# The last multiplications of the hybrid layer's mixer, from GpSimd to VectorE

## The chip, the cores and the metric

The kernel runs on one core of a Trainium2 chip. A core has TensorE (matrix products into PSUM), VectorE, ScalarE and GpSimd (elementwise work), and SyncE, which here issues most transfers. Each engine takes its own instructions in order, and the engines wait for each other through semaphores. The metric is the device time of one execution in microseconds; lower is better. Where several runs are shown, the median counts.

## The reference, cut to what matters

A network of two transformer layers and one hybrid layer is computed for 512 tokens of width 1024. The hybrid layer projects its input to p, gives slices of p to three mixers, and joins what they return:

```python
y_rwkv = rwkv7_time_mix(p_rwkv, ...)
y_mla = mla_attention(p_mla, ...)
y_gdn = gated_deltanet(p_gdn, ...)
y = jnp.concatenate([y_rwkv, y_mla, y_gdn], axis=-1)
h = h + y @ w_out[l]
```

Two of the mixers are recurrences. Each ends with a normalization of every head of 64 values and a multiplication by a gate:

```python
# rwkv7_time_mix
mean = jnp.mean(y, axis=-1, keepdims=True)
var = jnp.mean(jnp.square(y - mean), axis=-1, keepdims=True)
y = ((y - mean) * lax.rsqrt(var + RWKV_GN_EPS)).reshape(B, S, RWKV_WIDTH)
y = y * gn_g.astype(f32) + gn_b.astype(f32)
y = y + bonus.reshape(B, S, RWKV_WIDTH)
return (y * g.astype(f32)).astype(p.dtype)

# gated_deltanet
o = _rms(o, o_norm_g) * jax.nn.silu(hd(gate).astype(f32))
```

The change concerns the last multiplication of each, by `g` and by `silu(gate)`.

## The kernel before

Activations lie in SBUF transposed: a tile is 128 channels (partitions) by 512 tokens, in float32. The program is a row of stages. A stage allocates its tiles and semaphores, gives each engine a block of instructions, and ends with a barrier of all engines; in the trace, an engine's wait at such a barrier is put down to its sequencer and line 207. The order within a stage is written out by hand: each engine's instructions stand in program order, with a wait on a semaphore ahead of whatever depends on another instruction. The hybrid layer (`hybrid`) runs the stages that prepare both recurrences, then `recurrence` ("rec"), `mixer_ends` ("fin"), `latent` ("mla", the third mixer) and the output projection ("out"), then the feed-forward part.

`mixer_ends` treats six tiles in the order 3, 4, 5, 0, 1, 2. Tiles 0 to 2 are the first recurrence's, 3 to 5 are the gated delta net's. TensorE sums over heads by a product with a constant matrix (into `m_ps` for means, `v_ps` for squares). ScalarE makes the squares, the three gates `sgate` by Silu (semaphore `silued`), and then for each tile a logarithm and an exponential, which give the reciprocal root in `sq` (semaphore `rs_done`). VectorE computes the differences `d`, and then for each tile, as soon as its exponential is there:

- tiles 3 to 5: one instruction, line 2819, `o = y * o_norm * sq`;
- tiles 0 to 2: two instructions, line 2814, `o = d * gn_g * sq`, and, after a wait for it, line 2816, `o = (o + gn_b) + bonus`.

Each tile's last one counts up `o_done`. GpSimd waits for that and multiplies by the gate into `k.H`: line 2833 for tiles 3 to 5, with `sgate`, and line 2831 for tiles 0 and 1, with the gate that lies in `pi`. The sixth tile's multiplication, tile 2's, is VectorE's (line 2823). All operands of lines 2814 to 2833 lie in SBUF. `k.H` is read after the next barrier.

In `latent`, lines 3028 to 3041 are VectorE's first steps, 3047 takes TensorE's projections out of PSUM, 3062 and 3065 are the rotation of positions (3065 also waits for a product that GpSimd makes), and 3085 normalizes a block of attention weights, 4 blocks in each of 4 heads.

Of the kernel before, what the change touches and what calls it, by code (L numbers as in the profile page):

```python
# [19 lines left out]
ALU = mybir.AluOpType  # L20
# [27 lines left out]
MIX_T = 3  # L48
# [219 lines left out]
def linker(eng, sem):  # L268


    count = [0]

    def link(ins):
        ins.then_inc(sem, 1)
        count[0] += 1
        eng.wait_ge(sem, count[0])

    return link
# [1466 lines left out]
R_R, R_K, R_V, R_WA, R_G = 0, 3, 6, 9, 10  # L1745
# [1014 lines left out]
def mixer_ends(k, pi, y):  # L2760

    with Stage(k, "fin") as st:
        NP = 2 * MIX_T
        d = st.sb("d", [P, MIX_T, S])
        sq, o = (st.sb(n, [P, NP, S]) for n in ("sq", "o"))
        sgate = st.sb("sgate", [P, MIX_T, S])
        m_ps, v_ps = st.ps("m_ps", [P, MIX_T, S]), st.ps("v_ps", [P, 5, S])
        mean_done, d_done, squared, var_done, ln_done, rs_done, chain, o_done, out_done, silued = (st.sem(n) for n in (
            "mean_done", "d_done", "squared", "var_done", "ln_done", "rs_done", "chain", "o_done", "out_done", "silued"))

        order = [3, 4, 5, 0, 1, 2]
        with k.nc.Block() as block:
            @block.tensor
            def _(pe):
                for n in range(MIX_T):
                    pe.matmul(m_ps[:, n, :], k.c("heads"), y[n], start=True, stop=True).then_inc(mean_done, 1)
                for q, n in enumerate(order):
                    pe.wait_ge(squared, q + 1)
                    if q == 5:
                        pe.wait_ge(ln_done, 1)  # L2780
                    pe.matmul(v_ps[:, q % 5, :], k.c("heads"), sq[:, n, :], start=True, stop=True).then_inc(var_done, 1)

            @block.scalar
            def _(act):
                for n in order[:MIX_T]:
                    act.activation(sq[:, n, :], y[n], ACT.Square).then_inc(squared, 1)
                for j in range(MIX_T):
                    act.activation(sgate[:, j, :], pi[:, G_GATE + j, :], ACT.Silu).then_inc(silued, 1)
                for n in order[MIX_T:]:
                    act.wait_ge(d_done, n + 1)  # L2790
                    act.activation(sq[:, n, :], d[:, n, :], ACT.Square).then_inc(squared, 1)
                act.preload_act_table_set(LN_EXP)
                for q in range(NP + 1):
                    if q < NP:
                        n = order[q]
                        eps = 1 if n < MIX_T else 0
                        act.wait_ge(var_done, q + 1)
                        act.activation(sq[:, n, :], v_ps[:, q % 5, :], ACT.Ln, scale=1.0 / 64, bias=k.eps[:, eps:eps + 1]).then_inc(ln_done, 1)
                    if q:
                        n = order[q - 1]  # L2800
                        act.wait_ge(ln_done, q)
                        act.activation(sq[:, n, :], sq[:, n, :], ACT.Exp, scale=-0.5).then_inc(rs_done, 1)

            @block.vector
            def _(dve):
                link = linker(dve, chain)
                for n in range(MIX_T):
                    dve.wait_ge(mean_done, n + 1)
                    dve.scalar_tensor_tensor(out=d[:, n, :], in0=m_ps[:, n, :], scalar=-1.0 / 64, in1=y[n],
                                             op0=ALU.mult, op1=ALU.add).then_inc(d_done, 1)  # L2810
                for q, n in enumerate(order):
                    dve.wait_ge(rs_done, q + 1)
                    if n < MIX_T:
                        link(dve.scalar_tensor_tensor(out=o[:, n, :], in0=d[:, n, :], scalar=k.p("gn_g", n), in1=sq[:, n, :],
                                                      op0=ALU.mult, op1=ALU.mult))
                        dve.scalar_tensor_tensor(out=o[:, n, :], in0=o[:, n, :], scalar=k.p("gn_b", n), in1=pi[:, R_K + n, :],
                                                 op0=ALU.add, op1=ALU.add).then_inc(o_done, 1)
                    else:
                        dve.scalar_tensor_tensor(out=o[:, n, :], in0=y[n], scalar=k.p("o_norm"), in1=sq[:, n, :],
                                                 op0=ALU.mult, op1=ALU.mult).then_inc(o_done, 1)  # L2820

                dve.wait_ge(o_done, NP)
                dve.tensor_tensor(k.H[:, order[-1], :], o[:, order[-1], :], pi[:, R_R + order[-1], :], ALU.mult).then_inc(out_done, 1)

            @block.gpsimd
            def _(pool):
                pool.wait_ge(silued, MIX_T)
                for q, n in enumerate(order[:-1]):
                    pool.wait_ge(o_done, q + 1)
                    if n < MIX_T:  # L2830
                        pool.tensor_tensor(k.H[:, n, :], o[:, n, :], pi[:, R_R + n, :], ALU.mult).then_inc(out_done, 1)
                    else:
                        pool.tensor_tensor(k.H[:, 2 + n, :], o[:, n, :], sgate[:, n - MIX_T, :], ALU.mult).then_inc(out_done, 1)


TWO_PI = 2 * math.pi
# [277 lines left out]
def hybrid(k):  # L3114

    with ExitStack() as ctx:
        def sb(name, shape):
            return ctx.enter_context(k.nc.sbuf_tensor(name, shape, F32))

        pi = sb("pi", [P, IN_T, S])  # L3120
        with ExitStack() as ctx2:
            def sb2(name, shape):
                return ctx2.enter_context(k.nc.sbuf_tensor(name, shape, F32))

            bi = sb2("bi", [P, MIX_T, S])
            kr = sb2("kr", [P, MIX_T, TT, 2, P])
            ki = sb2("ki", [P, MIX_T, S])
            pc, el = sb2("pc", [P, MIX_T, NCH]), sb2("el", [P, MIX_T, NCH])
            rows2 = sb2("rows2", [P, S])
            cols = sb2("cols", [P, 120])  # L3130
            mixer_inputs(k, pi, kr, bi, ki, pc, rows2, cols)
            mt, n0 = sb2("mt", [P, 2 * MIX_T, NCH, CHUNK]), sb2("n0", [P, 2 * MIX_T, NCH, CHUNK])
            a, b = slice(0, MIX_T), slice(MIX_T, 2 * MIX_T)
            v, gk, gv = pi[:, R_V:R_V + MIX_T, :], pi[:, G_K:G_K + MIX_T, :], pi[:, G_V:G_V + MIX_T, :]
            rows = [pi[:, R_WA, :], pi[:, R_G, :], rows2]
            chunk_operators(k, "rwc", bi, kr, ki, v, kr, k.H, mt[:, a], n0[:, a], bi, v, pc)
            delta_rows(k, pi, kr, ki, rows, el)
            chunk_operators(k, "gdc", gk, kr, None, gv, ki, k.H, mt[:, b], n0[:, b], gk, gv, el, (rows, cols))
            y = [v[:, i, :] for i in range(MIX_T)] + [gv[:, i, :] for i in range(MIX_T)]
            recurrence(k, mt, n0, [bi[:, i, :] for i in range(MIX_T)] + [gk[:, i, :] for i in range(MIX_T)], (v, gv))  # L3140
        mixer_ends(k, pi, y)
        latent(k, pi)
# [125 lines left out]
```

## Time and profile before

| | |
|---|---|
| median of 3 runs | 2374.66 us |
| the three runs | 2374.49, 2374.66, 2376.17 us |
| the profiled execution | 2374.99 us |
| its span, first to last instruction | 2373.2 us |
| TensorE's mean granted clock | 0.972 |
| TensorE, VectorE, ScalarE busy | 2212.7, 1301.8, 913.2 us |
| GpSimd busy | 142.2 us, 113 instructions |
| stage "fin", from its first matmul to the first work behind its barrier | 1855.4 to 1877.6 us |

Durations and starts come from one profiled execution, whose time is 1.79 us longer than its span. A timeline lists instructions by their start in us from the start of the span; successive ones of one kind are merged, with their number behind x and their common duration. What an engine's idle time waited for stands in square brackets. The granted clock is a share of TensorE's full speed: 1.00 is 2.4 GHz, 0.50 is 1.2 GHz.

### The profile page before, as it was taken

What the parts mean: (1) busy time and instruction counts of PE and PEld (TensorE: products, weight loads), DVE (VectorE), ACT (ScalarE), POOL (GpSimd) and SP (SyncE); (2) the same over time, 40 slices, a digit from 0 to 9 for tenths busy, and PEclk for the clock granted to TensorE, in tenths of its full rate; (3) what the DMA queues carried; (4) which work ended last, traced back from release to release, by engine and by line L of the source; (5) the groups of instructions that cost most, each with busy time, mean ns of one, the idle gap of its engine ahead of it and who ended that gap; (6) DMA issues with size and microseconds to landing.
All of it is one profiled execution on the core that took longest, in us unless ns stands there. A gap on an engine that the chain in (4) does not pass through costs nothing. (4 is left out here: it accounts for less than half of the span.)

```text
span 2373.2 us, 35779 instructions
## 1 busy us (share of the span) xinstructions
PE 2212.7 (93%) x13998; PEld 1749.6 (74%) x13998; DVE 1301.8 (55%) x1703; ACT 913.2 (38%) x1428; POOL 142.2 (6%) x113
## 2 busy tenths in 40 slices
PE   7998999999989998999999999998777689999999
PEld 5786788888866776678888876777756337788887
DVE  5554476663476776386664376874343673533333
ACT  4444432222445565442222355552211452423222
POOL 0000011110000000011110000002222110000000
PEclk9998999999999999999999999999979889999999
DMA  6330333333223220323332323220000002333332
GB/s 229 99 125 18 107 96 99 90 101 96 94 61 107 69 70 26 101 86 97 94 101 98 95 67 94 80 89 2 3 2 3 13 1 72 111 96 96 98 96 71
DMA packets 52583, 186.96 MB, mean 79 GB/s; under 512 B 5712, under 2 KB 5968, under 8 KB 52336
## 3 DMA queue, kind: packets, MB, share of 16 engines
q1 hardware_dynamic: 52176, 184.69, 25.0%
q8 instruction: 87, 1.43, 0.2%
q10 hardware_dynamic: 288, 0.58, 0.1%
q14 instruction: 32, 0.26, 0.0%
HBM read 183.15 MB, written 2.10 MB: 78 GB/s over the span
## 5 line engine op out<-in xcount | busy, mean ns | idle before, releaser
L263 PE MATMUL tail_banks<-tail_r_hi,tail_w_hi 128*128 128x512 f32 x1344 | 529.8, 394 | 7.7 <-DVE tail_r_lo L1648 7.4
L265 PE MATMUL tail_banks<-tail_r_hi,tail_w_lo 128*128 128x512 f32 x1344 | 523.1, 389 | 0.0
L264 PE MATMUL tail_banks<-tail_r_lo,tail_w_hi 128*128 128x512 f32 x1344 | 523.1, 389 | 0.0
L263 PEld LDWEIGHTS tail_banks<-tail_r_hi,tail_w_hi 128*128 128x128 f32 x1344 | 252.2, 188 | 67.8 <-DVE tail_r_lo L1648 7.5
L264 PEld LDWEIGHTS tail_banks<-tail_r_lo,tail_w_hi 128*128 128x128 f32 x1344 | 252.3, 188 | 54.7 <-issue 3.4
L248 DVE TENSOR_TENSOR tail_w_lo<-ring,tail_w_hi 128x1024 fp32r<-128x1024 f32 x168 | 241.5, 1440 | 92.3 <-ACT tail_w_hi L242 89.1
L265 PEld LDWEIGHTS tail_banks<-tail_r_hi,tail_w_lo 128*128 128x128 f32 x1344 | 252.3, 188 | 53.0
L242 ACT ACTIVATE tail_w_hi<-ring 128x1024 fp32r<-128x1024 f32 x168 | 176.7, 1056 | 229.1 <-PE tail_banks L265 226.6
L263 PE MATMUL ff_banks<-ff_r_hi,ff_w_hi 128*128 128x512 f32 x512 | 200.0, 391 | 0.0
L265 PE MATMUL ff_banks<-ff_r_hi,ff_w_lo 128*128 128x512 f32 x512 | 199.2, 389 | 0.0
L264 PE MATMUL ff_banks<-ff_r_lo,ff_w_hi 128*128 128x512 f32 x512 | 199.2, 389 | 0.0
L705 POOL TENSOR_TENSOR tail_mid<-H 128x512 f32 x44 | 60.2, 1368 | 1202.6 <-ACT H L698 828.6
L248 DVE TENSOR_TENSOR ff_w_lo<-ring,ff_w_hi 128x1024 fp32r<-128x1024 f32 x64 | 78.4, 1226 | 61.3 <-ACT ff_w_hi L242 57.9
L263 PEld LDWEIGHTS ff_banks<-ff_r_hi,ff_w_hi 128*128 128x128 f32 x512 | 96.1, 188 | 20.6 <-issue 0.5
L264 PEld LDWEIGHTS ff_banks<-ff_r_lo,ff_w_hi 128*128 128x128 f32 x512 | 96.1, 188 | 20.2 <-issue 0.5
L265 PEld LDWEIGHTS ff_banks<-ff_r_hi,ff_w_lo 128*128 128x128 f32 x512 | 96.1, 188 | 20.0
L256 DVE TENSOR_TENSOR tail_r_lo<-tail_mid,tail_r_hi 128x512 fp32r<-128x512 f32 x44 | 30.4, 692 | 130.3 <-ACT tail_r_hi L252 130.3
L263 PE MATMUL na_acc<-na_r_hi,na_w_hi 128*128 128x512 f32 x192 | 78.1, 407 | 15.5 <-DVE na_r_lo L929 15.5
L263 PE MATMUL in_acc<-in_r_hi,in_w_hi 128*128 128x512 f32 x216 | 91.1, 422 | 0.0
L263 PE MATMUL da_acc<-da_r_hi,da_w_hi 128*128 128x512 f32 x192 | 80.8, 421 | 7.4 <-DVE da_r_lo L1250 7.4
L252 ACT ACTIVATE tail_r_hi<-tail_mid 128x512 fp32r (+1 forms) x44 | 27.7, 630 | 153.1 <-PE tail_banks L265 153.1
L265 PE MATMUL in_acc<-in_r_hi,in_w_lo 128*128 128x512 f32 x216 | 84.9, 393 | 0.0
(476 smaller groups left out, 3578.9 us busy)
## 6 DMA issues: line engine op xcount, KB each, us to landing
ring<-weights SPq DMA_DIRECT2D x315, 512.0 KB, 3.6
na_bias<-window_bias SPq DMA_DIRECT2D x16, 512.0 KB, 5.5
da_rel<-t_rel SPq DMA_DIRECT2D x8, 448.0 KB, 4.0
X<-xT SPq DMA_DIRECT2D x1, 2048.0 KB, 9.0
outT<-X SPq DMA_DIRECT2D x8, 256.0 KB, 2.1
const<-consts SPq DMA_DIRECT2D x1, 1328.5 KB, 14.4
tail_pt<-pT SPq DMA_DIRECT2D x2, 512.0 KB, 3.5
H<-lora ACTq DMA_DIRECT2D x1, 384.0 KB, 2.8
```

Of the source, the lines that this page charges most:

```text
L242: act.activation(self.w_hi[:, c % self.slots, :], k.ring[:, g % RING, :], ACT.Copy).then_inc(self.w_rounded, 1)
L248: dve.tensor_tensor(self.w_lo[:, c % self.slots, :], k.ring[:, g % RING, :], self.w_hi[:, c % self.slots, :].bitcast(F32), ALU.subtract).t ...
L252: act.activation(self.r_hi[:, slot, :], src, ACT.Copy).then_inc(self.rhs_rounded, 1)
L256: dve.tensor_tensor(self.r_lo[:, slot, :], src, self.r_hi[:, slot, :].bitcast(F32), ALU.subtract).then_inc(self.rhs_split, 1)
L263: pe.matmul(psum, hi, self.r_hi[:, rhs_slot, :], start=start, stop=False)
L264: pe.matmul(psum, hi, self.r_lo[:, rhs_slot, :], start=False, stop=False)
L265: return pe.matmul(psum, lo, self.r_hi[:, rhs_slot, :], start=False, stop=stop)
L705: pool.tensor_tensor(mid[:, f + j, :], gelu[:, j, :], value[:, j, :], ALU.mult).then_inc(mid_done, 1)
```

## The change

VectorE now does the multiplication by the gate for all six tiles, each right behind the instruction that makes its `o`. GpSimd's block in this stage is gone. The wait for the Silu gates is now on VectorE, one gate at a time. Nothing else differs.

```diff
--- before.py
+++ after.py
@@ -2818,19 +2818,12 @@
                     else:
                         dve.scalar_tensor_tensor(out=o[:, n, :], in0=y[n], scalar=k.p("o_norm"), in1=sq[:, n, :],
                                                  op0=ALU.mult, op1=ALU.mult).then_inc(o_done, 1)
-
-                dve.wait_ge(o_done, NP)
-                dve.tensor_tensor(k.H[:, order[-1], :], o[:, order[-1], :], pi[:, R_R + order[-1], :], ALU.mult).then_inc(out_done, 1)
-
-            @block.gpsimd
-            def _(pool):
-                pool.wait_ge(silued, MIX_T)
-                for q, n in enumerate(order[:-1]):
-                    pool.wait_ge(o_done, q + 1)
+                    dve.wait_ge(o_done, q + 1)
                     if n < MIX_T:
-                        pool.tensor_tensor(k.H[:, n, :], o[:, n, :], pi[:, R_R + n, :], ALU.mult).then_inc(out_done, 1)
+                        dve.tensor_tensor(k.H[:, n, :], o[:, n, :], pi[:, R_R + n, :], ALU.mult).then_inc(out_done, 1)
                     else:
-                        pool.tensor_tensor(k.H[:, 2 + n, :], o[:, n, :], sgate[:, n - MIX_T, :], ALU.mult).then_inc(out_done, 1)
+                        dve.wait_ge(silued, n - MIX_T + 1)
+                        dve.tensor_tensor(k.H[:, 2 + n, :], o[:, n, :], sgate[:, n - MIX_T, :], ALU.mult).then_inc(out_done, 1)
```

VectorE's rows at the end of the stage "fin", with the lines of each kernel's own file; `fin_` marks the stage's tiles:

```order
 L2809 SCALAR_TENSOR_TENSOR fin_d<-fin_m_ps,pi 128x512 x3
-L2819 SCALAR_TENSOR_TENSOR fin_o<-pi,par,fin_sq 128x512 x3
+L2819 SCALAR_TENSOR_TENSOR fin_o<-pi,par,fin_sq 128x512
+L2826 TENSOR_TENSOR H<-fin_o,fin_sgate 128x512
+L2819 SCALAR_TENSOR_TENSOR fin_o<-pi,par,fin_sq 128x512
+L2826 TENSOR_TENSOR H<-fin_o,fin_sgate 128x512
+L2819 SCALAR_TENSOR_TENSOR fin_o<-pi,par,fin_sq 128x512
+L2826 TENSOR_TENSOR H<-fin_o,fin_sgate 128x512
 L2814 SCALAR_TENSOR_TENSOR fin_o<-fin_d,par,fin_sq 128x512
 L2816 SCALAR_TENSOR_TENSOR fin_o<-fin_o,par,pi 128x512
+L2823 TENSOR_TENSOR H<-fin_o,pi 128x512
```

A multiplication stands between any two tiles now, where VectorE went on to the next tile at once; tiles 0 and 1 have theirs as tile 2 had it.

GpSimd's rows from the end of the stage before "fin" to the stage "mla" (ISA rows belong to the clearing of semaphores between stages):

```order
-L206 ISA x2
-L2825 UNCONDITIONAL_BRANCH
-L2833 TENSOR_TENSOR H<-fin_o,fin_sgate 128x512 x3
-L2831 TENSOR_TENSOR H<-fin_o,pi 128x512 x2
-L2772 UNCONDITIONAL_BRANCH
-L206 ISA
-L3014 UNCONDITIONAL_BRANCH
-L3018 COPY mla_qk<-pi 32x512 x4
-L3022 TENSOR_TENSOR mla_qk<-mla_qk,mla_cs 32x512 x8
-L2873 UNCONDITIONAL_BRANCH
 L206 ISA x3
```

The five multiplications and their block are gone; the rows of "mla" below stand in the changed kernel too, seven line numbers lower.

## Rows read from the trace of the kernel before

**Rows 1.** Page, busy us of two engines, share of the span, instructions.

```profile
PE 2212.7 (93%) x13998; PEld 1749.6 (74%) x13998; DVE 1301.8 (55%) x1703; ACT 913.2 (38%) x1428; POOL 142.2 (6%) x113
```

**Rows 2.** Timeline of TensorE: start us, duration us, engine, instruction [idle before].

```profile
1863.78 1.10 PE L2781 MATMUL fin_v_ps<-fin_sq,const 128*128 128x512 f32 x2 [1.15 <-ACT fin_sq L2798]
1880.11 2.08 PE L2884 MATMUL mla_a_ps<-mla_sq,const 128*128 128x512 f32 x2 [15.24 <-ACT mla_sq L2960]
```

**Rows 3.** Timeline of VectorE, from the first exponential to the barrier.

```profile
1864.76 0.75 DVE L2819 SCALAR_TENSOR_TENSOR fin_o<-pi,par,fin_sq 128x512 f32<-128x512 f32 x1 [5.77 <-ACT fin_sq L2802]
1865.86 2.28 DVE L2819 SCALAR_TENSOR_TENSOR fin_o<-pi,par,fin_sq 128x512 f32<-128x512 f32 x2 [0.34 <-ACT fin_sq L2802]
1868.06 1.75 DVE L2814 SCALAR_TENSOR_TENSOR fin_o<-fin_d,par,fin_sq 128x512 f32<-128x512 f32 x1
1869.85 1.63 DVE L2816 SCALAR_TENSOR_TENSOR fin_o<-fin_o,par,pi 128x512 f32<-128x512 f32 x1
1871.40 0.74 DVE L2814 SCALAR_TENSOR_TENSOR fin_o<-fin_d,par,fin_sq 128x512 f32<-128x512 f32 x1
1872.18 1.63 DVE L2816 SCALAR_TENSOR_TENSOR fin_o<-fin_o,par,pi 128x512 f32<-128x512 f32 x1
1873.74 0.74 DVE L2814 SCALAR_TENSOR_TENSOR fin_o<-fin_d,par,fin_sq 128x512 f32<-128x512 f32 x1
1874.51 1.63 DVE L2816 SCALAR_TENSOR_TENSOR fin_o<-fin_o,par,pi 128x512 f32<-128x512 f32 x1
1876.18 0.69 DVE L2823 TENSOR_TENSOR H<-fin_o,pi 128x512 f32<-128x512 f32 x1
```

**Rows 4.** Instructions of tile fin_o, line 2819: ns min/median/max, first and last start.

```profile
L2819 DVE SCALAR_TENSOR_TENSOR fin_o<-pi,par,fin_sq x3: 737/751/1620, 1864.8 to 1867.4; 128x512 f32<-128x512 f32 x3
```

**Rows 5.** Timeline of GpSimd in the stage "fin".

```profile
1865.66 1.27 POOL L2833 TENSOR_TENSOR H<-fin_o,fin_sgate 128x512 f32<-128x512 f32 x1 [39.75 <-DVE fin_o L2819]
1867.56 3.38 POOL L2833 TENSOR_TENSOR H<-fin_o,fin_sgate 128x512 f32<-128x512 f32 x2 [0.63 <-DVE fin_o L2819]
1871.56 1.70 POOL L2831 TENSOR_TENSOR H<-fin_o,pi 128x512 f32<-128x512 f32 x1 [0.63 <-DVE fin_o L2816]
1873.89 1.70 POOL L2831 TENSOR_TENSOR H<-fin_o,pi 128x512 f32<-128x512 f32 x1 [0.63 <-DVE fin_o L2816]
```

**Rows 6.** Timeline of ScalarE: the second, fifth and sixth of the six exponentials.

```profile
1865.19 0.64 ACT L2802 ACTIVATE fin_sq<-fin_sq 128x512 f32<-128x512 f32 x1
...
1868.45 1.18 ACT L2802 ACTIVATE fin_sq<-fin_sq 128x512 f32<-128x512 f32 x2
```

**Rows 7.** Timeline of VectorE: the first instruction behind the barrier, three merged.

```profile
1877.66 2.37 DVE L3028 TENSOR_SCALAR mla_cg<-pi,par 128x512 f32<-128x512 f32 x3 [0.79 <-PEq L207]
```

**Rows 8.** Windows: us, length, TensorE busy (instructions), granted clock, DMA share, GB/s.

```profile
1880.00:1886.00 6.00, 5.49 (x6) 0.53 0.15 58
...
1916.00:1937.00 21.00, 16.02 (x35) 0.51 0.00 1
...
1960.00:1964.00 4.00, 3.91 (x20) 0.59 0.00 0
...
1970.00:2373.00 403.00, 396.86 (x1738) 1.00 0.31 94
```

**Rows 9.** Timeline of VectorE: the rotation, no pause between.

```profile
1922.18 0.68 DVE L3062 TENSOR_TENSOR mla_t<-mla_a_ps,mla_sn 32x512 f32<-32x512 f32 x1
1922.89 0.68 DVE L3065 TENSOR_TENSOR mla_qk<-mla_qk,mla_t 32x512 f32<-32x512 f32 x1
```

**Rows 10.** Timeline of VectorE: first projection taken out of PSUM.

```profile
1888.51 0.69 DVE L3047 TENSOR_TENSOR mla_qk<-mla_a_ps,mla_rs 96x512 f32<-96x512 f32 x1 [1.74 <-PE mla_a_ps L2898]
```

**Rows 11.** Timeline of VectorE: first normalized block of heads 0, 1 and 3.

```profile
1928.41 0.29 DVE L3085 TENSOR_SCALAR mla_e<-mla_e,mla_inv 128x128 f32<-128x128 f32 x1
...
1937.35 0.29 DVE L3085 TENSOR_SCALAR mla_e<-mla_e,mla_inv 128x128 f32<-128x128 f32 x1
...
1954.09 0.29 DVE L3085 TENSOR_SCALAR mla_e<-mla_e,mla_inv 128x128 f32<-128x128 f32 x1
```

## Prediction, made before the changed kernel had run

> **What bounds the kernel now.** I read four views in this order. The page's busy times show TensorE at 93% of the span and GpSimd at 6% [rows 1]: the kernel is TensorE's, except where TensorE has nothing to do. The timeline of the end of the mixer shows such a place. TensorE's last matmul of the stage "fin" ends at 1863.78 + 1.10 = 1864.88 us, and its next one, in the stage "mla", starts at 1880.11, after 15.24 us of idle time [rows 2]. So in this stretch the time is set by the chain on VectorE, not by TensorE. The third view is VectorE's own timeline: it works from 1864.76 to 1876.18 + 0.69 = 1876.87 with one pause, of 0.34 us [rows 3]. GpSimd is done at 1873.89 + 1.70 = 1875.59 [rows 5], that is 1.28 us before VectorE; ScalarE at 1868.45 + 1.18 = 1869.63 [rows 6]. VectorE is therefore the last to reach the barrier between the stages, and its first instruction behind it starts at 1877.66, 0.79 us later [rows 7]. What moves VectorE's end moves the start of "mla" by as much. The fourth view, the windows, shows whether something behind swallows it: from 1970 us to the end TensorE is busy 396.86 of 403 us [rows 8], so nothing there waits for another clock than TensorE's, and a stage that starts earlier ends the kernel earlier.
>
> **What VectorE and GpSimd do to each other now.** The same instruction has two durations here. The three of line 2819 take 737, 751 and 1620 ns [rows 4]; line 2814 takes 1.75 us once and 0.74 us twice; line 2816 takes 1.63 us three times [rows 3]. The long durations are five, and each of them ends shortly after a GpSimd instruction ends. GpSimd's five end at 1866.93, 1869.27, 1870.94, 1873.26 and 1875.59 (start plus duration; the two merged ones are 3.38 us together) [rows 5]. The long VectorE instructions end at 1867.48, 1869.81, 1871.48, 1873.81 and 1876.14 [rows 3, 4]. The distance is 0.54 or 0.55 us in all five. I read this as follows: a VectorE instruction that takes two operands from SBUF and begins while GpSimd works there waits until GpSimd is done, and only then streams. The short ones of line 2814 began at 1871.40 and 1873.74, 0.16 and 0.15 us ahead of a GpSimd instruction. So the multiplications given to GpSimd are not done beside VectorE's work; VectorE stands still for most of each of them.
>
> **The change, step by step.** (a) Five long instructions become short. At 0.74 us for a free one [rows 3] the excess is 1.62 - 0.74 = 0.88, 1.75 - 0.74 = 1.01 and 3 x (1.63 - 0.74) = 2.67, together 4.56 us less. (b) Five multiplications come to VectorE. The one that it does already, from SBUF to SBUF with GpSimd idle, takes 0.69 us, and starts 0.04 us behind the end of the instruction on which it waits (1876.14 to 1876.18) [rows 3]. So 5 x 0.73 = 3.65 us more. (c) Before an independent instruction VectorE starts 0.08 us before the last has ended (1871.40 against 1871.48) [rows 3]; there is one more such place now, 0.08 us less. (d) The pause before 1865.86, from 1865.51, in which VectorE waited for ScalarE's second exponential [rows 3, 6], is filled by the first multiplication: 0.35 us less. The sum is -4.56 + 3.65 - 0.08 - 0.35 = **-1.34 us**.
>
> Walked forward instead, it is the same: 1864.76 + 0.75 + 0.04 + 0.69 = 1866.24 for the first tile, twice 1.39 for the next two (-0.08 + 0.74 + 0.04 + 0.69), and three times 2.17 for those with two steps ahead of the multiplication (-0.08 + 0.74 + 0.04 + 0.74 + 0.04 + 0.69): 1875.53 instead of 1876.87. ScalarE does not become the bound: its second exponential is ready at 1865.83 and the last at 1869.63 [rows 6], and VectorE wants them at 1866.16 and 1873.28.
>
> (e) Added waits. Behind each wait for o_done stands only VectorE's own next work, and the producer is the instruction just ahead, which the 0.04 us covers. The second wait, for silued, stands before three of the multiplications. ScalarE's gates are computed before its first exponential, so it is satisfied. Two waits in a row, one of them long satisfied, cost nothing visible where the trace has them: line 3065 waits for VectorE's line 3062 and for GpSimd, and starts at 1922.89 behind 1922.18 + 0.68 [rows 9]. I take 0; the upper bound is another 0.04 for each, 0.12 us. (f) GpSimd loses its block and comes to the barrier early; nobody waits for it. Its next work starts with everyone else's. (g) No DMA moves past another: the loads of "mla" are issued by SP behind the same barrier, so they start 1.34 us earlier too.
>
> **A rule weighed.** In the stretch from 1864.76 to 1876.87 VectorE is busy nearly all the time, and the row says that moving work away from it brought it 4.56 us of standing still for 3.65 us of work saved. The Trainium skill, Perfetto Trace Analysis, section Optimizing Scalar/DVE Operations, says that with VectorE saturated it may make sense to offload some work to ScalarE or even GpSimd, and warns that between VectorE and GpSimd it might not help. By its first half this change would lose; by its warning and by the rows it gains. The first half is rival 1 below.
>
> **Rivals.** 1, *the long durations are VectorE's own* (slower than before). If the five long durations stay when GpSimd is idle, only (b), (c) and (d) are left: 3.65 - 0.08 - 0.35 = +3.22 us, 2377.9. It decides where less than 3.22 of the 4.56 us goes away. Against it stands that lines 2819 and 2814 show both durations with one shape. The partial form is stronger: line 2816 is never seen free, 1.63 us three times [rows 3], and could be so by itself. Then 2.67 us of (a) stays, and the sum is +1.33 us, 2376.0. Against it: all three end 0.54 or 0.55 us behind GpSimd, as the other two long ones do. The Trainium skill, SBUF — State Buffer, section SBUF: two separate sides, calls the pair of ports an exclusive lock, held for a whole instruction, on which the loser blocks fully. By that rule line 2816 is a blocked one, and the distances in the trace agree.
>
> 2, *TensorE's clock* (either sign). TensorE's granted clock is 0.53 in 1880 to 1886, at the lower of its two levels (1.2 GHz), 0.51 in 1916 to 1937, and 0.59 in 1960 to 1964 [rows 8]; before each of these it had been idle or partly idle. The whole of "mla" moves by 1.34 us, and where the clock falls and rises may move otherwise. Bounds from the rows. At the start the matmuls run at the lower level; with the full clock the next step of VectorE, which waited 1.74 us for TensorE [rows 10], gains at most that. In 1960 to 1964 TensorE is the bound, and about 3.4 us at the lower level are at most 1.7 us lost. In the heads between, the first one takes 1937.35 - 1928.41 = 8.94 us mostly at the lower level, the next two (1954.09 - 1937.35) / 2 = 8.37 at the full one [rows 11]: 0.57 us a head. So the clock can give at most 1.74 + 1.7 + 0.57 = 4.0 us (2369.3, all three falls gone) and take some 3 x 0.57 = 1.7 us (2375.0).
>
> 3, *the gain does not arrive*: another engine holds the barrier. Nothing speaks for it; the next to arrive is GpSimd at 1875.59, and its work is what the change takes away. It gives 2374.7.
>
> **How the numbers follow.** The profiled execution took 2374.99 us, 1.79 more than its span; with the sum it is 2373.65. The median of the three runs is 0.33 lower, and the forecast is 2374.66 - 1.34 = 2373.3 us. A measurement of this kernel tells about 0.2%, 4.7 us, from no change. Chances: the forecast with clock effects under 2 us 0.78; a clock that moves in its favour by more 0.08, 2370; one against it 0.05, 2375.5; rival 1 in its partial form 0.03, in full 0.02; rival 3 0.04. The range runs from 2370.4 (the forecast, the first clock gain and most of one of the others) to 2375.8 (the forecast, 1.7 us of lost clock and the 0.8 us by which the three runs stand apart from their middle). Faster by over 0.2% needs more than the clock's full gain or something not seen here, 0.06; slower by over 0.2%, 0.05; within, 0.89.
>
> **What would show it.** In the profile after: lines 2819, 2814 and 2816 all at 0.74 to 0.75 us, six multiplications at 0.69 us, VectorE without a pause from 1864.76, its last end near 1875.5, and the first work of "mla" near 1876.3. A line 2816 at 1.63 us with GpSimd idle would prove rival 1. A start of "mla" 1.3 us earlier with an end of the kernel that differs by another amount would be rival 2, and the granted clock would show where. The prediction is wrong if work ahead of 1864 us moves, since nothing there is changed.

## The result, and the profile after

The changed kernel takes 2377.97 us (median of 20 runs, 2375.02 to 2385.74) against 2374.89 us for the kernel before (median of 20 runs, 2370.47 to 2379.10). The ratio is 1.0016, with an interval of 1.0010 to 1.0023: it is slower by 3.1 us by the medians (3.8 by the ratio), where 1.3 us of gain was forecast, and it lies outside the range. Its profiled execution took 2378.00 us with a span of 2376.2.

The stage that was changed does what the prediction said, to a hundredth. VectorE's timeline of the changed kernel: the first of the three tiles with one step ahead of the multiplication, the first and the end of the last of the three with two, and the first work behind the barrier (start us, duration us, line; [idle before]), answering [rows 3]:

```profile
1864.42 0.75 DVE L2819 SCALAR_TENSOR_TENSOR fin_o<-pi,par,fin_sq 128x512 f32<-128x512 f32 x1 [5.77 <-ACT fin_sq L2802]
1865.20 0.69 DVE L2826 TENSOR_TENSOR H<-fin_o,fin_sgate 128x512 f32<-128x512 f32 x1
...
1868.59 0.75 DVE L2814 SCALAR_TENSOR_TENSOR fin_o<-fin_d,par,fin_sq 128x512 f32<-128x512 f32 x1
1869.37 0.75 DVE L2816 SCALAR_TENSOR_TENSOR fin_o<-fin_o,par,pi 128x512 f32<-128x512 f32 x1
1870.16 0.69 DVE L2823 TENSOR_TENSOR H<-fin_o,pi 128x512 f32<-128x512 f32 x1
...
1873.72 0.75 DVE L2816 SCALAR_TENSOR_TENSOR fin_o<-fin_o,par,pi 128x512 f32<-128x512 f32 x1
1874.51 0.69 DVE L2823 TENSOR_TENSOR H<-fin_o,pi 128x512 f32<-128x512 f32 x1
1876.31 2.37 DVE L3021 TENSOR_SCALAR mla_cg<-pi,par 128x512 f32<-128x512 f32 x3 [1.11 <-PEq L207]
```

Line 2816, never seen free before, takes 0.75 us where it took 1.63. From the first exponential to VectorE's last end there are 1875.20 - 1864.42 = 10.78 us, before 12.11: 1.33 us less, forecast 1.34. The barrier behind it takes 0.32 us of that away again: 1.11 us of idle time where [rows 7] has 0.79.

The loss lies behind. The first instruction of "fin" lies 0.34 us earlier in this trace, though nothing ahead of it was changed, so I count from VectorE's first instruction in "fin" (line 2809, at 1856.58 before and 1856.24 after). The table gives the start of VectorE's first instruction of each part, from the timelines, in us from there:

| part | before | after | difference |
|---|---|---|---|
| "mla" begins | 21.08 | 20.07 | -1.01 |
| first projection taken out of PSUM | 31.93 | 29.77 | -2.16 |
| first normalization | 44.87 | 42.71 | -2.16 |
| last step of the rotation | 68.23 | 71.58 | +3.35 |
| head 0, first block | 71.83 | 75.18 | +3.35 |
| head 3, first block | 97.51 | 100.86 | +3.35 |
| output projection | 111.84 | 115.19 | +3.35 |

The rotation of positions takes 5.51 us more, and nothing else takes more: 3.35 us behind the mark less 0.34 ahead of it are the 3.01 us by which the two profiled executions differ. TensorE's windows of both kernels say why (us, length, TensorE busy (instructions), granted clock, DMA share, GB/s). Before:

```profile
1886.00:1902.00 16.00, 14.96 (x36) 1.00 0.00 0
1902.00:1916.00 14.00, 12.08 (x29) 1.00 0.00 1
1916.00:1936.00 20.00, 15.02 (x31) 0.51 0.00 1
```

After:

```profile
1880.00:1886.00 6.00, 5.13 (x10) 0.85 0.00 0
1886.00:1902.00 16.00, 14.91 (x37) 1.00 0.00 0
1902.00:1916.00 14.00, 14.00 (x18) 0.51 0.00 1
1916.00:1936.00 20.00, 16.71 (x26) 0.50 0.01 1
1936.00:1940.00 4.00, 3.89 (x14) 0.52 0.00 0
```

The clock falls to its lower level (1.2 GHz) at 1902.2 instead of 1916.3, 14 us earlier, and rises at 1939.8 instead of 1936.8. (In return it had risen 3.0 us after TensorE's restart in "mla" instead of 5.5, which is the second microsecond gained in the table, and the clock gain that rival 2 named.) At the lower level the matmuls of a rotation step take nearly twice as long (1.91 and 2.02 us for 1.04 and 1.10), and TensorE becomes the bound. TensorE's timeline before, at 1.00:

```profile
1906.40 1.04 PE L2909 MATMUL mla_a_ps<-mla_qk,const 32*32 32x512 f32 x2
1907.38 1.10 PE L2915 MATMUL mla_s_ps<-mla_sq,const 96*96 96x512 f32 x2
1908.40 1.04 PE L2909 MATMUL mla_a_ps<-mla_qk,const 32*32 32x512 f32 x2
1909.38 1.10 PE L2915 MATMUL mla_s_ps<-mla_sq,const 96*96 96x512 f32 x2
1911.06 1.01 PE L2909 MATMUL mla_a_ps<-mla_qk,const 32*32 32x512 f32 x2 [0.58 <-DVE mla_t L3062]
```

After, at 0.50, without a pause:

```profile
1905.36 1.91 PE L2902 MATMUL mla_a_ps<-mla_qk,const 32*32 32x512 f32 x2
1907.20 2.02 PE L2908 MATMUL mla_s_ps<-mla_sq,const 96*96 96x512 f32 x2
1909.15 1.91 PE L2902 MATMUL mla_a_ps<-mla_qk,const 32*32 32x512 f32 x2
```

From one rotation matmul to the next there are 1909.15 - 1905.36 = 3.79 us, where before they were 2.45 us apart once VectorE set the pace (1911.06 to 1913.51). VectorE, which had no idle time in these steps before, now waits in each step for GpSimd's product, and GpSimd for TensorE:

```profile
1904.97 0.68 DVE L3058 TENSOR_TENSOR mla_qk<-mla_qk,mla_t 32x512 f32<-32x512 f32 x1 [0.51 <-POOL mla_qk L3015]
1908.78 0.68 DVE L3058 TENSOR_TENSOR mla_qk<-mla_qk,mla_t 32x512 f32<-32x512 f32 x1 [0.79 <-POOL mla_qk L3015]
```

### The profile page after: what moved, and what is told of

It is laid out like the page before. It is cut to its first block and busy times, and to the rows that moved or that the text cites. A ratio compares the mean times of both kernels' runs of the same rounds, so it can differ in the third digit from the quotient of the medians.

```text
span 2376.2 us, 35781 instructions
## 1 busy us (share of the span) xinstructions
PE 2219.7 (93%) x13998; PEld 1750.1 (74%) x13998; DVE 1297.2 (55%) x1708; ACT 913.2 (38%) x1428; POOL 133.9 (6%) x108
```

## The experiments

Two theories. **C, the clock**: the change gains in its own stage and loses because TensorE's clock falls at another point of the rotation, since "mla" starts at another moment. **G, the change itself**: something that it does (GpSimd idle for 50 us, instructions at other addresses) makes "mla" slower, whenever it starts.

### The start of "mla" put back: e1, e2

Behind the last multiplication of "fin", VectorE does two more, whose results are not used:

```diff
+dve.tensor_tensor(sq[:, 3, :], o[:, 3, :], o[:, 3, :], ALU.mult).then_inc(extra, 1)
+dve.tensor_tensor(sq[:, 4, :], o[:, 4, :], o[:, 4, :], ALU.mult).then_inc(extra, 1)
```

In the changed kernel:

> The changed kernel with two further VectorE multiplications of 128x512 behind the last one of the stage fin (their results are not used). They take 2 x 0.61 us, so the stage mla starts about where it starts in the kernel before. Theory C (clock): the loss of 3 us is not made by the change in its own stage, which gains its 1.3 us, but by TensorE's clock, which falls at 1902 instead of 1916 us because mla starts at another moment. Then this kernel is near the kernel before, 2374 to 2376 us, and the clock falls in the second half of the rotation. Theory G (the change itself, such as GpSimd being idle longer or the instructions lying elsewhere): the loss stays and the delay is added to it, 2379.2 us.

Measured: 2375.49 us median of 12 runs; ratio to the kernel before, beside it, 1.0003 (0.9994 to 1.0012). More work made the changed kernel faster by 2.5 us. Its trace repeats the kernel before within 0.13 us at every mark: "mla" at 20.96, first projection 31.81, last rotation step 68.10, head 0 71.70, output projection 111.77 us after the first instruction of "fin" (before: 21.08, 31.93, 68.23, 71.83, 111.84). The clock falls at 1917.8, 59.7 us behind that mark as before. Its windows:

```profile
1886.00:1902.00 16.00, 15.13 (x35) 0.96 0.00 0
1902.00:1916.00 14.00, 11.93 (x29) 1.00 0.00 1
1916.00:1936.00 20.00, 14.51 (x29) 0.55 0.01 1
```

GpSimd takes no part in "fin" here, and the program is the changed kernel's but for two more instructions. So theory G falls as a cause of the 3 us. The barrier, too, is back at 0.79 us:

```profile
1877.59 0.69 DVE L2828 TENSOR_TENSOR fin_sq<-fin_o 128x512 f32<-128x512 f32 x1
1879.07 2.37 DVE L3023 TENSOR_SCALAR mla_cg<-pi,par 128x512 f32<-128x512 f32 x3 [0.79 <-PEq L207]
```

In the kernel before:

> The kernel before with the same two further VectorE multiplications at the end of the stage fin, so that mla starts 1.2 us later with GpSimd's work in place. Theory G: the delay and nothing else, 2376.1 us. Theory C: the delay moves mla against the clock's falls, so the time is 2376.1 plus or minus up to 5 us, the sign being open, and where it differs the mean granted clock differs with it, 0.966 to 0.974.

Measured: 2375.30 us, ratio 1.0005 (0.9995 to 1.0015). That is 0.8 us below what the delay alone would give; both theories allow it. In the trace "mla" begins 1.21 us later (22.29) and the first projection only 0.66 later: the clock rises 29.0 us behind the mark in both, so sooner after TensorE's restart here.

### The clock held in the rotation: e3, e4

One more matmul ahead of each rotation's, into a free bank of PSUM:

```diff
 def rotate(n):
+    pe.matmul(fill[:, 0:256], k.c("ones"), k.const[:, 0:256], start=True, stop=True)
     pe.wait_ge(s["qn"], n + 1)
```

> The changed kernel with one more matmul of full array size, 256 columns (0.43 us at the full clock), into a free PSUM bank ahead of each of the eight rotations in mla, where TensorE waits for VectorE. Theory C: the extra work keeps the clock at 1.00 through the rotation, whose steps take 2.45 us instead of 3.79, and the kernel takes 2371 to 2373 us. If the clock falls all the same, each step is 0.9 us longer than 3.79 and the kernel takes 2380 or more. Theory G: 2378 or more, whatever the clock.

Measured: 2372.39 us, as theory C expected and 5.6 us below the changed kernel's median, by adding work to TensorE. The clock stays up until 1918.5, and the last rotation step starts at 66.33 instead of 71.58. The windows:

```profile
1902.00:1916.00 14.00, 13.44 (x36) 1.00 0.00 1
1916.00:1936.00 20.00, 16.14 (x42) 0.57 0.01 1
```

> The kernel before with the same eight matmuls ahead of the rotations. Theory C: with the clock held in both, the difference between this kernel and the changed one with them is the gain of the change alone, 1.0 to 1.4 us, and this one takes 2372.5 to 2374.5 us. Theory G: this one is faster than the changed one with them by 3 us.

Measured: 2375.48 us, 3.1 us above the changed kernel with the same fillers, where 1.0 to 1.4 were expected. A miss of size. The sign is what theory C says, and against theory G: with the rotation kept at the full clock, the change gains. But the pair is not clean. In the traces "mla" begins 1.01 us later here (21.08 against 20.07), as it should; another 1.15 us come in by the first projection, because the clock rises 2.4 us later after TensorE's restart; the rotation adds 0.24, and the heads 0.5, where it is low for longer. So the clock had to be held in all of "mla".

### The clock held everywhere behind 1864 us: e6, e7, f1, f2

Besides the filler ahead of each rotation (512 columns for the last two): eleven matmuls of 128x512 behind the last one of "fin", two at the start of "mla", three ahead of the heads.

> The changed kernel with filler matmuls wherever TensorE idles in fin and mla: eleven of 128x512 behind the last one of fin (their PSUM bank is free), two at the start of mla, one of 256 columns ahead of each of the first six rotations and of 512 ahead of the last two, three of 512 ahead of the heads. Theory C: the granted clock stays at 1.00 from 1864 us to the end, the first steps of mla and the first head run at the full clock, and the kernel takes 2369.5 to 2371.5 us. Theory G: nothing of this helps by more than 1 us against the changed kernel with fillers in the rotation alone (2372.4).

Measured: 2370.84 us, ratio 0.9980 (0.9969 to 0.9992), inside what was expected, though the clock still fell once, at 1953.1.

> The kernel before with the same filler matmuls. Theory C: with the clock at 1.00 in both, what is left between the two is what the change does in its own stage, 1.0 to 1.4 us, so this one takes 2370.7 to 2372.9 us. If the difference is far from that, something besides VectorE's chain and the clock is moved by the change.

Measured: 2372.90 us, ratio 0.9990 (0.9979 to 1.0001): 2.1 us above e6, more than the 1.4 expected. In its trace the clock fell in the longer end of "fin" (1877.1 to 1880.5) and twice in the heads, so again the pair differs in more than "fin". Two more kernels close these gaps: twelve fillers at the end of "fin" in the changed kernel and thirteen in the kernel before, and one in each head:

```diff
+keep_busy(pe, k, m_ps[:, 0, :], 12)        # at the end of fin; 13 in the kernel before
...
+if i == 2:
+    keep_busy(pe, k, fill[:, :], 1)
 pe.wait_ge(s["w_done"], g + 1)
```

> The changed kernel with the filler matmuls of the run before it, one more at the end of fin (twelve) and one of 512 columns in each of the four heads, where TensorE waits longest for VectorE. It should hold the granted clock at 1.00 from 1864 us to the end, which the fillers so far did not in the heads (a fall at 1953 us). Theory C: 2367 to 2370 us, and with the next kernel it isolates the change.

> The kernel before with the same fillers and thirteen at the end of fin, since fin is longer there. Theory C: with the clock at 1.00 from 1864 us on in both traces, the time from the first instruction of VectorE in fin to the first in the output projection is longer here by what fin alone gives, 1.0 to 1.4 us, and the medians differ by about as much. Theory G: the changed kernel is not ahead, or is ahead by something else than that.

Measured: 2367.14 us (10 runs), ratio to the kernel before 0.9971 (0.9962 to 0.9980), and 2370.03 us (12 runs), ratio 0.9983 (0.9974 to 0.9992). The medians are 2.9 us apart, where 1.0 to 1.4 were expected: a second miss of size. The traces say what the difference is made of. The windows of the changed one, whose clock does not fall behind 1864 us:

```profile
1880.00:1886.00 6.00, 5.13 (x13) 1.00 0.00 0
1886.00:1902.00 16.00, 14.92 (x40) 1.00 0.00 1
1902.00:1916.00 14.00, 13.86 (x35) 1.00 0.01 1
1916.00:1936.00 20.00, 17.36 (x69) 1.00 0.00 0
```

and of the kernel before with fillers, which has one short fall, at 1923.4:

```profile
1902.00:1916.00 14.00, 12.91 (x37) 1.00 0.01 2
1916.00:1936.00 20.00, 18.18 (x51) 0.91 0.00 0
```

| us from the first instruction of "fin" | f1 (changed) | f2 (before) | difference |
|---|---|---|---|
| "mla" begins | 20.07 | 21.10 | -1.03 |
| first projection | 29.14 | 30.04 | -0.90 |
| first normalization | 41.45 | 42.36 | -0.91 |
| last step of the rotation | 65.31 | 66.25 | -0.94 |
| head 0 | 68.46 | 70.10 | -1.64 |
| output projection | 104.52 | 106.16 | -1.64 |

Up to the fall in f2 the clocks are equal, and the change is worth 0.9 to 1.0 us: the 1.33 of its own stage less the 0.32 at the barrier. The other 0.7 us in the table is f2's fall. The medians can't be read as finely: the two profiled executions are 6.56 us apart, and 4.88 of them lie ahead of "fin", where the programs are the same (its first instruction starts at 1855.17 and 1860.05). f1 is also the fastest kernel here, 7.6 us below the kernel before. The fillers alone (f2) give 4.7 of it; of the other 2.9 the traces put 0.9 to 1.0 down to the change.

### The start of "mla" at other moments: e8, e9

One, and four, further multiplications behind the last one of the changed kernel.

> The changed kernel with one further VectorE multiplication at the end of fin (0.61 us), so that mla starts between the changed kernel (3 us slower than before) and the one with two of them (like before). Theory C: the time doesn't follow the delay but the clock: either the early fall comes, and the kernel takes 2378.6 us, or the late one, and it takes 2374.8 us. A value in the middle in all runs, such as 2376.7, would speak against it.

Measured: 2378.56 us median of 12, ratio 1.0011 (1.0000 to 1.0022). The runs form two groups, six at 2373.9 to 2376.4 (mean clock 0.971 to 0.973) and six at 2380.8 to 2383.1 (0.966 to 0.968). No run lies in the middle, but the second group is 2 to 4.5 us above the 2378.6 expected for the early fall. The trace is of that group: the clock falls at 1906.9, 46.3 us behind the first instruction of "fin", nearly as in the changed kernel (46.0), and the output projection starts 115.57 us behind it (115.19 there). So this execution has the early fall, and what it takes beyond the changed kernel lies ahead of the change: "fin" begins at 1860.57, 4.33 us later, and the clock was at the lower level from 1838.7 to 1848.9. That the first group has the late fall is read from its times alone; no trace of it was taken.

> The changed kernel with four further VectorE multiplications at the end of fin (2.44 us), so that mla starts about 1.1 us later than in the kernel before, as in the kernel before with two of them (2375.3 us). Theory C: the same start gives the same falls of the clock, 2375 to 2376 us, whether or not GpSimd takes part in fin. Theory G: 2378.0 + 2.4 = 2380.4 us.

Measured: 2380.90 us median of 12, ratio 1.0017 (1.0005 to 1.0030). The median is a miss for theory C and near theory G's 2380.4. Again there are two groups: three runs at 2371.7 to 2372.2 (clock 0.974), nine at 2379.0 to 2383.4 (0.968 and 0.969). The trace was of the first, and follows e2's marks: "mla" 22.15, last rotation step 69.74, output projection 112.60 (e2: 22.29, 69.85, 112.71). Three runs 8 us below its value speak against theory G, but the others needed a trace of their own. Part of the short time is luck ahead of the change: "fin" begins at 1852.73 in this trace, 3.85 us earlier than in the kernel before.

> A second look at the changed kernel with four further multiplications, whose runs lay either at 2372 us (clock 0.974, where the trace was taken) or at 2379 to 2383 (0.968 or 0.969). Theory C: if this execution is one of the long ones, its trace shows VectorE's stretch in fin unchanged and a stretch of mla at the clock of 0.50 that is longer by 10 us or more, with rotation steps of 3.8 us. Theory G: the excess shows at the clock of 1.00 as well.

Measured: one execution, 2381.59 us. The same program as e9, and the same up to the first normalization (45.41 and 45.47 us behind the first of "fin"); then the clock falls 49.5 us behind it instead of 56.2. The last rotation step starts at 73.74 instead of 69.74, the output projection at 119.32 instead of 112.60. As theory C expected, the rotation's steps take 3.79 us (1910.80 to 1914.59), and the low stretch is 10.2 us longer (1905.2 to 1942.7 against 1908.9 to 1936.2). First e9's windows:

```profile
1902.00:1916.00 14.00, 13.42 (x23) 0.75 0.00 1
1916.00:1936.00 20.00, 15.86 (x39) 0.50 0.00 1
1936.00:1940.00 4.00, 4.00 (x20) 0.97 0.00 0
1940.00:1970.00 30.00, 23.78 (x121) 1.00 0.06 18
```

then those of e9_again:

```profile
1902.00:1916.00 14.00, 13.51 (x20) 0.61 0.00 1
1916.00:1936.00 20.00, 17.00 (x25) 0.50 0.00 0
1936.00:1940.00 4.00, 3.61 (x13) 0.50 0.02 4
1940.00:1970.00 30.00, 26.09 (x122) 0.84 0.00 1
```

With nothing changed in the program, the earlier fall is worth 4.0 us by the end of the rotation. Another 2.7 come in by the output projection, with two further falls in the heads (1949.6 and 1966.6), 6.7 in all. The last 3.0 of the 9.7 us between the two executions lie ahead of "fin", which begins at 1855.72 and 1852.73, though VectorE was within 0.15 us in both at 1735: e9_again has two falls there, at 1772.1 and 1782.3, where e9's trace has none. This is the strongest evidence for theory C, and it corrects it: a start of "mla" doesn't fix the place of the fall. The two groups of times suggest that it sets how often which place is taken; with one or two traces of a kernel that is not shown.

### The changed kernel once more

> The changed kernel once more, beside the others on the same chip. Theory C: its times lie on the same line over the mean granted clock as those of the kernel before (2373.5 at 0.973, 2380.1 at 0.968), only at other places on it; median 2376 to 2380 us. Theory G: at an equal mean clock it is 3 us above the kernel before.

Measured: 2380.07 us median of 5 runs (2377.86 to 2386.09), just above the range of theory C and 2.1 above the first median of the same program; ratio 1.0033 (1.0020 to 1.0046). The trace repeats the first one's marks within 0.04 us, the fall at 46.1 us among them. Over all runs beside the experiments, by the mean granted clock: the kernel before has 41 of 92 runs at 0.973 with a mean of 2373.6 us, 22 at 0.972 with 2375.5 and 17 at 0.968 with 2380.1; the changed one has 14 of 25 at 0.971 with 2377.6 and five at 0.969 with 2379.4. The line through 2373.6 and 2380.1 has 2376.2 at 0.971 and 2378.8 at 0.969. The changed kernel lies 1.4 and 0.6 us above it, so neither "on the line" nor "3 us above it" holds. A mean clock says how long it was low, not whether TensorE was the bound there; the traces say that.

## Why the prediction was wrong

- **What bounds the stage: right.** VectorE's chain in "fin" set the start of "mla". That the start moves by as much as VectorE's end was wrong by 0.32 us: 1.33 became 1.01.
- **Steps (a) to (d), -1.34 us: right**, 1.33 measured. The reading that five long VectorE instructions waited for GpSimd is borne out by line 2816's 0.75 us. The Trainium skill, SBUF — State Buffer, section SBUF: two separate sides, speaks of an exclusive lock; the trace agrees, since with GpSimd idle all nine are at 0.74 to 0.75 us.
- **Steps (e) and (f): right in "fin"**, each multiplication starts 0.03 or 0.04 us behind its producer, also with the second wait. That "its next work starts with everyone else's" held too (GpSimd at 1876.29, VectorE at 1876.31 us).
- **Rival 1: did not occur**, in either form.
- **Rival 2, the clock: the right mechanism, and the step that failed.** Its loss was bounded by 3 x 0.57 = 1.7 us, from the heads [rows 11], and a loss of more than 2 us was put at a chance of 0.05, although that bound already excluded it. The stretch where the clock costs most, the rotation, was left out of the bound. The kernel before had been at the lower level only in the last steps of it, when each has one pair of matmuls left (2.46 and 2.66 us a step, hardly more than 2.45). A full step has two pairs, 1.91 + 2.02 us at the lower level less their overlap, and takes 3.79. The first five steps take 18.84 us (1901.69 to 1920.53) instead of 11.79 (1904.18 to 1915.97), 7.05 more; the last two, back to back, give 1.5 back, which makes the 5.51. The rows for it were in the trace of the kernel before: the two pairs of a step, back to back, go from 1906.40 to 1908.40, 2.00 us. At half the rate that is an estimate of 4.0 us, more than the 2.45 of a step, so TensorE had to become the bound. Five such steps are 20.0 us instead of 11.79, and a bound of -1.34 + 8.2 = +6.9 us would have held the result (+3.1). The chance of a loss from the clock had to be far more than 0.05, since the rows showed three falls in the 100 us behind the change.
- **The gain at the start of "mla": right in kind**, bounded by 1.74 us and measured as 2.16 - 1.01 = 1.15.
- **"The prediction is wrong if work ahead of 1864 us moves": too strict a sign.** "fin" began 0.34 us earlier with nothing changed there, and e9's program began it at 1852.73 and at 1855.72 us in two executions.

The forecast took the kernel's answer to an earlier start as a shift. With the clock held (f1 and f2) it is one, of 0.9 to 1.0 us.

## What to carry to other kernels

Where TensorE's clock falls and rises within the program, a gain or loss of a microsecond ahead of it says little about the whole: first mark the stretches at the lower clock, and work out for the next ones what a step costs at half the rate, by doubling the time of its matmuls and asking whether they then exceed the step. If they do, that excess times the number of steps belongs in the range with a real chance. Fillers that hold the clock were worth more than the small edit (4.7 us against 1 here), and they are also what makes the traces of a pair comparable behind the change. The medians still hold whatever the clock did ahead of it.

## What the runs showed of the hardware that was not expected

- TensorE can be busy without a pause and stay at the lower clock: 14.00 of 14 us in 1902 to 1916 at 0.51, with matmuls almost all over 32 and 96 rows. With one matmul over 128 rows added to each step (e3), the same stretch ran at 1.00, busy for 13.44 of 14 us.
- The clock's fall in the idle time of "fin" came at nearly the same place in every trace without fillers there, 11.8 to 12.2 us behind the first instruction of "fin". The other falls did not, ahead of the change either: the kernel before has one at 1803.7 and none at 1772, the changed kernel one at 1772.6 and none at 1804. In the rotation they differ even for one program (49.5 and 56.2 us). The Trainium skill, TensorE: Matmul & The Clock Gate, section Part 1: The HAM clock gate, calls the clock gate's timing free-running and reports other numbers of slow matmuls in different runs of the same kernel. The pair of e9 agrees that one program changes at different points; that the free-running timing is the reason no run here shows.
- The 0.32 us at the barrier remain open. The idle time between VectorE's last instruction and its next is 1.11 us in the changed kernel (twice), in f1, in e3 and in e6, 0.93 in e8, but 0.79 in e1, in e9 and e9_again, and 0.79 or 0.80 in the kernels with GpSimd's work. GpSimd's part in "fin" is not what decides it, since e1 and e9 have none; the idle time is shorter where VectorE ends later. Something else that is ready at a fixed moment does not fit as it stands: in e8 VectorE ends 19.55 us behind the first instruction of "fin", and a moment at 20.07, where "mla" starts in the changed kernel, would leave it 0.79 and not 0.93. The cause stays open.
